# Value pages of a paged cache: issued by SyncE in one line with the key pages, instead of by GpSimd

## What is computed

```python
past_k = cache_k[l][page_table].reshape(b, -1, SB_HEADS, SB_HEAD_DIM)
past_v = cache_v[l][page_table].reshape(b, -1, SB_HEADS, SB_HEAD_DIM)
...
z = jnp.einsum('bqhd,bkhd->bhqk', qi, k) * scale + hb
log_keep = jnp.where(mask, jax.nn.log_sigmoid(-z), 0.0)
later = lax.cumsum(log_keep, axis=3, reverse=True) - log_keep
w = jnp.where(mask, jnp.exp(jax.nn.log_sigmoid(z) + later), 0.0)
return jnp.einsum('bhqk,bkhd->bqhd', w, v)
```

## Time and profile before

| | us |
|---|---|
| median of 3 runs (3461.80 to 3471.36) | 3466.26 |
| the profiled execution | 3464.99 |
| its span, first to last instruction | 3463.3 |
| mix stage, layer 0, about 338 to 637 of the span | 299 |
| mix stage, layer 1, about 2035 to 2333 | 298 |

### The profile page before, as it was taken

One profiled execution on the slowest core, in us unless ns is written; L12 is line 12 of the kernel. 1 busy time (PEld: TensorE's weight loads), 2 busy tenths in 40 slices (PEclk: granted clock), 3 DMA queues, 4 the chain that ended last, 5 costly groups with the idle time before them and its releaser, 6 DMA issues.

```text
span 3463.3 us, 62725 instructions
## 1 busy us (share of the span) xinstructions
PE 3249.3 (94%) x23775; PEld 3048.2 (88%) x23775; DVE 1920.3 (55%) x3351; ACT 1337.2 (39%) x1640; POOL 379.1 (11%) x465
## 2 busy tenths in 40 slices
PE   5999899889999999999889988979899999999995
PEld 4999566789999999999889975649899999999994
DVE  5574555356654665466366655453666446645654
ACT  2453565333433333233245535552344333333331
POOL 2000554020000000000010025530200000000000
PEclk8999899889999999999999999999899999999997
DMA  5442699634444444444444347985344444444441
GB/s 155 136 133 87 216 303 303 206 113 139 152 146 153 150 145 150 154 146 134 129 126 135 122 126 234 320 280 168 107 152 145 147 155 146 146 152 151 145 136 44
DMA packets 467532, 553.10 MB, mean 160 GB/s; under 512 B 20043, under 2 KB 413868, under 8 KB 466624
## 3 DMA queue, kind: packets, MB, share of 16 engines
q1 hardware_dynamic: 436354, 461.42, 41.6%
q0 software_dynamic: 26112, 88.93, 8.0%
q10 hardware_dynamic: 4898, 0.55, 0.1%
HBM read 534.46 MB, written 16.38 MB: 159 GB/s over the span
## 4 chain that ended last, share of the span: by engine, by line
PE 89%; DVE 5%; ACT 3%; DMA 1%; issue 1%; ACTq 1%; DVEq 0%; POOL 0%; POOLq 0%
PE ps L917 25%; PE ps L918 25%; PE ps L919 25%; PE ps L1094 3%; PE ps L1134 2%; DVE hl L1372 2%; PE ps L1104 1%; PE ps L1253 1%; PE ps L1243 1%; PE ps L1180 1%; PE ps L1237 1%; DMA xrow<-in_x_sample 0%; PE ps L1116 0%; ACT wz L785 0%; ACT kT L763 0%
## 5 line engine op out<-in xcount | busy, mean ns | idle before, releaser
L1330 DVE TENSOR_TENSOR wl<-raw,wh 128x1024 fp32r<-128x1024 f32 (+1 forms) x752 | 897.6, 1202 | 1098.9 <-ACT wh L640 1091.9
L640 ACT ACTIVATE wh<-raw 128x1024 fp32r<-128x1024 f32 (+1 forms) x752 | 781.2, 1041 | 1680.5 <-PE ps L919 1678.2
L917 PE MATMUL ps<-hh,wh 128*128 128x320 f32 x4224 | 1319.8, 312 | 21.7 <-DVE hl L1372 18.0
L919 PE MATMUL ps<-hh,wl 128*128 128x320 f32 x4224 | 1314.2, 311 | 0.0
L918 PE MATMUL ps<-hl,wh 128*128 128x320 f32 x4096 | 1275.0, 311 | 0.0
L917 PEld LDWEIGHTS ps<-hh,wh 128*128 128x128 f32 x4224 | 800.0, 189 | 30.4 <-issue 12.3
L919 PEld LDWEIGHTS ps<-hh,wl 128*128 128x128 f32 x4224 | 800.4, 189 | 0.0
L918 PEld LDWEIGHTS ps<-hl,wh 128*128 128x128 f32 x4096 | 776.6, 190 | 0.0
L917 PE MATMUL ps<-ah,wh 128*128 128x320 f32 x1408 | 435.8, 310 | 0.1
L919 PE MATMUL ps<-ah,wl 128*128 128x320 f32 x1408 | 435.6, 309 | 0.0
L918 PE MATMUL ps<-al,wh 128*128 128x320 f32 x1408 | 435.6, 309 | 0.0
(11 more groups left out here) (321 smaller groups left out, 3010.4 us busy)
## 6 DMA issues: line engine op xcount, KB each, us to landing
raw<-in_w_gate SPq DMA_DIRECT2D x88, 1024.0 KB, 5.1
raw<-in_w_up SPq DMA_DIRECT2D x88, 1024.0 KB, 5.1
raw<-in_w_in SPq DMA_DIRECT2D x72, 1024.0 KB, 5.2
kring<-in_cache_k SPq DMA_DIRECT2D x256, 256.0 KB, 4.2
vring<-in_cache_v POOLq DMA_DIRECT2D x256, 256.0 KB, 4.7
raw<-in_w_down SPq DMA_DIRECT2D x64, 1024.0 KB, 5.4
raw<-in_w_out SPq DMA_DIRECT2D x32, 1024.0 KB, 5.4
raw<-in_w_down SPq DMA_DIRECT2D x32, 768.0 KB, 4.8
```

The source lines that it names most:

```text
L640: act.activation(wh[:, s % 2, half, :], raw[:, s, half, :], ACT.Copy).then_inc(hi_done, 1)
L917: pe.matmul(out, wh[:, s % 2, kk, w], hi(row), start=first, stop=False)
L919: mm = pe.matmul(out, wl[:, s % 2, kk, w], hi(row), start=False, stop=last)
L1330: dve.tensor_tensor(wl[:, s % 2, half, :], raw[:, s, half, :], wh[:, s % 2, half, :].bitcast(F32), ALU.subtract).then_inc(lo_done, 1)
```

## The change

`value_in` moves from POOL's program to SP's. Its DMA, its ring, its page and its wait for `v_used` stay as they are. In SP's program a value page of chunk 0 stands behind each key page of chunk 1, and a value page of chunk q - 2 behind each key page of chunk q from q = 3 on; the last two chunks of values follow after the last key page, ahead of the weight units of the out projection. The first value page waits for PE, ACT and DVE to have ended the input projection (POOL had that wait from its `meet`). POOL's program loses the eight pages of chunk 0 ahead of the copy and the page in each slot from chunk 2 to 16.

```diff
+                def value_in(q, k):
+
+                    if q:
+                        sync.wait_ge(v_used, l * (CHUNKS * 8) + (8 * (q - 1) + k + 1))
+                    elif k == 0:
+                        for eng in ("pe", "act", "dve"):
+                            sync.wait_ge(at_stage[eng], stage(l, M_IN))
+                    at_page = (q // 4 * 2 + k // 4) * PAGES + 4 * (3 - q % 4) + k % 4
+                    page = sync.value_load(pages[0:1, at_page:at_page + 1], min_val=0,
+                                           max_val=a["cache_v"].shape[1] - 1)
+                    sync.dma_start(vring[:, k, :], a["cache_v"][l, page].rearrange("s h d -> s (h d)")
+                                   ).then_inc(v_loaded[k], 16)
+
                 for q in range(CHUNKS):
                     for k in range(RING):
...
                         sync.dma_start(kring[:, k, :], a["cache_k"][l, page].rearrange("s h d -> s (h d)")
                                        ).then_inc(k_loaded[k], 16)
+                        if q == 1:
+                            value_in(0, k)
+                        if q >= 3:
+                            value_in(q - 2, k)
                         if slot == SLOT["y", 1, 3] + 2:
                             state_in(0)
...
+                for q in (CHUNKS - 2, CHUNKS - 1):
+                    for k in range(RING):
+                        value_in(q, k)
 
                 def out_unit(s, i):
...
-                def value_in(q, k):
-
-                    if q:
-                        pool.wait_ge(v_used, l * (CHUNKS * 8) + (8 * (q - 1) + k + 1))
-                    at_page = (q // 4 * 2 + k // 4) * PAGES + 4 * (3 - q % 4) + k % 4
-                    page = pool.value_load(pages[0:1, at_page:at_page + 1], min_val=0, max_val=a["cache_v"].shape[1] - 1)
-                    pool.dma_start(vring[:, k, :], a["cache_v"][l, page].rearrange("s h d -> s (h d)")
-                                   ).then_inc(v_loaded[k], 16)
...
-                for k in range(RING):
-                    value_in(0, k)
                 pool.tensor_copy(ptmp[:].rearrange("p g (b t) -> p g b t", b=NB), xps[:, :, :, NT:]).then_inc(ptail_in, 1)
                 pool.wait_ge(kv_stored, l * 64 + 64)
                 for qn in range(CHUNKS + 3):
                     for k in range(8):
                         slot = 8 * qn + k
-                        if 2 <= qn <= CHUNKS:
-                            value_in(qn - 1, k)
```

## The result

The changed kernel takes 3512.45 us (median of 4 runs) against 3467.24 us for the kernel before on the same chip: a ratio of 1.0131, 95% interval 1.0113 to 1.0149. Slower was forecast, but 3479 us and at most 3500. The profiled execution of the changed kernel has a span of 3511.1 us, 47.8 us over that of before. In the changed kernel the lines from the page reads on stand 8 lower: the key pages are L411 and L413, the value pages L398 and L400, step "s" is L1212, PE's transposes of key pages L1102 and its value products L1142.

What follows compares the result with a forecast made beforehand. SP's issuing, 17.6 us a chunk against PE's 16.7, was to bound the mix stages: 3464.99 + 6 + 5 for the two layers = 3476, with longer issues 3479 us, POOL's gain already included; range 3453 to 3500.

Steps and rivals of the forecast that it cites:

- the mechanism: In the mix stages two pages a slot cost SP 2.20 us against PE's 2.09, so SP sets the pace.
- POOL's term: Without the pages POOL's last tail store goes out earlier, ending PE's wait in step "s": 12 to 16 us gained.
- the end of the stage: Out projection weight units now stand behind the last value page: 0.4 us more in layer 0, at worst 2.
- 1.10 us a page: SP's time per page in a full line; 223 steps from key page (3, 0) to the last value page, 245.3 us.
- states and the rest: Eight state loads between SP's pages add 7.2 us, slower pages behind three of them 0.7 us, in each layer.
- The extra cost of a page: Longer page issues on SP's fuller queue: 0.007 us a page, bounds 0 and 0.25, 1.5 us a layer.
- what PE waits for: In the mix stages PE waits for key and value pages (`kring`, `vring`), from about chunk 9 on.
- SP keeps up: Rival 1: a pair of pages costs SP no more than 2.09 us, the line never fills: 3450 us; chance 0.12.
- Near cancelling: Rival 2: states don't hold SP's line and pages land at once: 3466 to 3476 us; chance 0.25.
- The stores not earlier: Rival 3: POOL's tail stores stay late, or SP loses the gain waiting for PE: 3493 us; chance 0.13.
- The one queue holds SP: Rival 4: state loads and pages on one full queue stop SP, 0.05 us a page: 3501 us; chance 0.08.

Runs made afterwards that it cites:

- e1: The changed kernel with the value pages' places as program constants instead of table reads, same DMAs, order and waits: 3449.26 us, ratio 0.9960.
- e2: The kernel before, with two more table reads on SP behind each key page from chunk 3 on, values still on POOL: 3508.42 us, ratio 1.0128.
- e3: The kernel before, with only value chunks 0 and 1 issued by SP and chunks 2 to 15 by POOL: 3450.16 us, ratio 0.9963.
- e10: The changed kernel with the loads of states 1, 2 and 3 issued three key pages apart instead of as one block: 3508.85 us, ratio 1.0118.
- e4: The changed kernel with a quarter of each value page read, as many DMAs, table reads and waits: 3502.28 us, ratio 1.0110.
- e5: The changed kernel with POOL's stores of sample states cut to 8 of 128 partitions: 3501.02 us, ratio 1.0092.
- e8: The kernel before, with value chunks 0 to 5 issued by SP and 6 to 15 by POOL: 3476.93 us, ratio 1.0025.

## Why the prediction was wrong, point by point

**Right: the mechanism.** SP's line fills at key page (3, 0), and from chunk 4 on SP waits no more; e1 and e2 show that its time, and nothing else that was moved, makes the difference.

**Right: POOL's term.** The last tail store was forecast for 385.6 and goes out at 383.48; the wait in step "s" is 0.4 us in layer 0 and none in layer 1. The term was put at 12 to 16 us; e3 measures 12.

**Right: the end of the stage.** The weight unit was to add 0.4 us; from the last value page's end (654.79 for 634.33) to the first matmul of the out projection (659.72 for 639.01) it is 4.9 us for 4.7.

**Wrong: 1.10 us a page.** That is the median step, and it was right as a median (1.10 and 1.11). But a line that is never empty pays the mean. SP's line, taken apart by its instructions one by one:

| from key page (3, 0) to the last value page, us | forecast | layer 0 | layer 1 |
|---|---|---|---|
| 223 page steps of 1.10 | 245.3 | 245.3 | 245.3 |
| table reads over 0.268 | 0 | 9.5 | 10.2 |
| page issues over 0.333 | 1.5 | 5.6 | 5.0 |
| eleven gaps with 0.30 more | 0 | 3.3 | 3.3 |
| states and the rest | 7.9 | 6.4 | 9.3 |
| sum | 254.7 | 270.1 | 273.1 |

So the line was forecast 15.4 and 18.4 us too short. It began 1.9 us earlier than forecast in layer 0 and, measured from the end of layer 0, 2.4 us later in layer 1. The stage's ends move by 7.5 - 1.9 + 15.4 = 21.0 and 6.5 + 2.4 + 18.4 = 27.3 us by this; in the traces by 20.7 (first out projection matmul) and about 28. The extra cost of a page was put at 0.007 us, between 0 and 0.25; the first three rows of excess make it 18.4 / 223 = 0.083 us.

The trace of before held a warning. In its two mix stages the 202 table reads on SP from 380 us and 2095 us on have a mean of 0.328 us against the median of 0.268 of the earlier trace rows, and each of the sixteen state stores has exactly one slow read, 1.6 to 3.1 us behind its issue. The 256 issues of key pages have a mean of 0.345 us for a median of 0.333. Slow reads cost nothing before, because SP stood waiting for PE anyway. With these means a page is 0.072 us dearer, 16 us a layer, and 3476 becomes 3508. That this comes so near 3512 is in part luck: the slow reads go with POOL's stores, and there are no more of these after, so over twice as many reads gave 31 slow ones for 19. A read came out only 0.043 and 0.046 us dearer instead of 0.060, while issues came out 0.025 and 0.022 us dearer instead of 0.012, and the longer gaps add 0.015. One of those reads, 2.6 us behind a store's issue, from the kernel before:

```profile
L398 SPq TENSOR_LOAD <-pages x1: 725/725/725, 520.5 to 520.5; - x1
```

**Wrong in part: what PE waits for.** Pages were named, from chunk 9 on. They are waited for (key pages 17.3 us and value pages 24.7 us, both layers together), but the first long wait is for a state, in chunk 8. How long that chunk is didn't move the time (e10).

**The rivals.** SP keeps up: fell; e1 shows what it would have taken, a page without its read. Near cancelling: fell. The stores not earlier: fell, they were. The one queue holds SP was nearest in time (3501) with 0.05 us a page, but issues carry 5.0 to 5.6 us a layer, half of that; and with a quarter of the value bytes the kernel is still at 1.0110 (e4). The range ended at 3500, because it left out the upper half of this rival and put no spread on the 1.10.

## What to carry to other kernels

Before work is moved to an engine that looks idle, add up its instructions for one period of the loop and compare that with the bottleneck's period, and use means, not medians: an engine that waits hides its slow instructions, and one that never waits pays each of them. If the sum comes near the period (here 17.6 us a chunk by medians, for 16.7), move only the part that pays: here two chunks of sixteen took the whole gain (0.37%) and none of the loss. And what stands in an issuing line has a lead of its own; look first at the item with the least of it, in most of these runs a state load.

## What the runs showed of the hardware that was not expected

- A table read on SP takes 0.26 to 0.28 us, but up to 1.5 us while a store of 512 KB from the same memory is under way (1.7 us once, behind POOL's tail stores); with stores of a sixteenth of that the long ones under them nearly vanish (e5). In the mix stages of before and after all 50 reads over 0.32 us from key page (3, 0) on, 19 and 31, start during a store by POOL.
- A full line on SP has one gap between instructions that is 0.34 us instead of 0.03 to 0.06 every 128 instructions (eleven in each layer of the changed kernel). The cause is open.
- A key page issued behind three loads of 512 KB lands after 10.9 us, where the means of the other chunks are 3.0 to 5.5 (e8).
- Behind a wait of 6.1 us PE worked 7 us at a granted clock of 0.50 (e8).
- Landing got shorter, not longer, with both pages on SP's queue: 3.0 and 3.1 us in the median, for 4.2 and 4.7 before. The traffic is thinner too (258 GB/s for 298); in e1, with the same queue and a line that is not full, it is 3.9 and 4.3 us.
